# Attention of layer 1: a second output bank in the early steps, and a new order of values, low parts, swaps and ropes

## What is computed

```python
def sink_attend(q, k, v, sink, mask):
    s = jnp.einsum('...qkgd,...jkd->...kgqj', q, k).astype(jnp.float32) * (C_DH ** -0.5)
    if mask is not None:
        s = jnp.where(mask, s, -jnp.inf)
    sk = jnp.broadcast_to(sink.astype(jnp.float32)[:, :, None, None], s.shape[:-1] + (1,))
    p = jax.nn.softmax(jnp.concatenate([s, sk], axis=-1), axis=-1)[..., :-1]
    return jnp.einsum('...kgqj,...jkd->...qkgd', p.astype(v.dtype), v)

def odd_mixer(h, pos, k_cache, v_cache, w_in, b_in, w_out, sink):
    z = h @ w_in + b_in
    q, k, v = ...                      # 16 query heads, 2 key/value heads, 64 wide
    q, k = rope(q, pos), rope(k, pos)
    ...                                # each chunk of 64 queries sees 192 keys
    return o @ w_out, ...
```

## Time and profile before

| | us |
|---|---|
| median of 3 runs | 2476.39 (2475.01 to 2478.08) |
| profiled execution | 2472.65 |
| its span | 2470.9 |
| attention of layer 1, scores of batch 0 to the first product after the attention | 1411.9 to 1603.1 |
| PE busy over the span | 2385.7 |
| DVE, ACT, POOL busy over the span | 1408.4, 816.2, 216.2 |

### The profile page before, as it was taken

The page is one execution under the profiler, slowest core; times in us unless marked ns, Lnnn a source line. Parts: engine busy times, 40 slices in busy tenths (PEclk is TensorE's granted clock), DMA queues, the critical chain, the costliest instruction groups (busy, mean ns, idle before and its releaser), DMA issues.

```text
span 2470.9 us, 36737 instructions
## 1 busy us (share of the span) xinstructions
PE 2385.7 (97%) x15073; PEld 2296.2 (93%) x15073; DVE 1408.4 (57%) x2008; ACT 816.2 (33%) x1473; POOL 216.2 (9%) x147
## 2 busy tenths in 40 slices
PE   8998898999999999999999879999999999999998
PEld 7998677999999999999999857799999999999998
DVE  4445666665555655555574466666455555555557
ACT  5323566432222222222245465443222222222224
POOL 3435001000000000000040032200000000000003
PEclk9999999999999999999999989999999999999999
DMA  5112100211111111111002100021111111111101
GB/s 154 53 52 73 32 14 10 69 52 52 51 51 34 35 50 34 51 51 51 18 8 75 32 6 17 21 69 54 49 51 51 34 51 34 38 46 51 51 1 74
DMA packets 108291, 110.98 MB, mean 45 GB/s; under 512 B 3448, under 2 KB 98079, under 8 KB 108204
## 3 DMA queue, kind: packets, MB, share of 16 engines
q1 hardware_dynamic: 103268, 107.30, 13.7%
q10 hardware_dynamic: 4936, 2.47, 0.4%
HBM read 99.92 MB, written 9.42 MB: 44 GB/s over the span
## 4 chain that ended last, share of the span: by engine, by line
PE 89%; DVE 5%; ACT 3%; issue 1%; POOL 1%; DMA 0%; SPq 0%; ACTq 0%; POOLq 0%; DVEq 0%
PE PS L234 76%; PE PS L2395 2%; PE PS L1986 2%; PE PS L369 1%; PE PS L2377 1%; PE PS L2020 1%; PE PS L2332 1%; PE PS L2004 1%; PE PS L2227 1%; DVE nm L1414 1%; PE PS L2176 1%; DVE m L1697 1%; ACT E L1189 1%; ACT zs_e L828 1%; PE PS L1917 0%
## 5 line engine op out<-in xcount | busy, mean ns | idle before, releaser
L234 PE MATMUL PS<-xhi,uphi_f 128*128 128x364 f32 x2064 | 456.5, 330 | 0.9 <-issue 0.9
L234 PE MATMUL PS<-xhi,uplo_f 128*128 128x364 f32 x2064 | 455.1, 329 | 0.0
L234 PE MATMUL PS<-xlo,uphi_f 128*128 128x364 f32 x2064 | 455.1, 329 | 0.0
L234 PEld LDWEIGHTS PS<-xhi,uphi_f 128*128 128x128 f32 x2064 | 357.7, 188 | 2.4 <-issue 1.5
L234 PEld LDWEIGHTS PS<-xlo,uphi_f 128*128 128x128 f32 x2064 | 357.8, 188 | 0.0
L234 PEld LDWEIGHTS PS<-xhi,uplo_f 128*128 128x128 f32 x2064 | 357.8, 188 | 0.0
L1618 DVE TENSOR_TENSOR resid<-PS,resid 128x728 f32<-128x728 f32 x320 | 216.8, 720 | 181.6 <-PE PS L234 181.6
L234 PE MATMUL PS<-hhi_f,dhi_f 128*128 128x364 f32 (+1 forms) x1008 | 222.9, 330 | 2.2 <-DVE hlo_f L1289 2.2
L234 PE MATMUL PS<-hhi_f,dlo_f 128*128 128x364 f32 (+1 forms) x1008 | 222.9, 330 | 0.0
L234 PE MATMUL PS<-hlo_f,dhi_f 128*128 128x364 f32 (+1 forms) x1008 | 222.7, 329 | 0.0
L1028 ACT COPY edge<-ext_f 128x4 f32 (+1 forms) x86 | 17.1, 199 | 530.3 <-DVE ext_f L1544 530.3
(11 more groups left out here) (312 smaller groups left out, 3426.2 us busy)
## 6 DMA issues: line engine op xcount, KB each, us to landing
graw<-in_w_up SPq DMA_DIRECT2D x22, 1024.0 KB, 5.1
vraw<-in_w_up SPq DMA_DIRECT2D x22, 1024.0 KB, 5.1
draw<-in_w_down SPq DMA_DIRECT2D x22, 1024.0 KB, 5.0
wraw<-in_w_in_even SPq DMA_DIRECT2D x16, 512.0 KB, 4.1
wraw<-in_w_in_odd SPq DMA_DIRECT2D x10, 512.0 KB, 4.4
out_y_prompt<-yN SPq DMA_DIRECT2D x8, 512.0 KB, 2.7
xnat<-in_x_prompt SPq DMA_DIRECT2D x3, 1024.0 KB, 6.7
out_diff_k_prompt<-kNat ACTq DMA_DIRECT2D x4, 512.0 KB, 3.4
```

The costliest lines, as they stand in the source:

```text
L234: last = nc.tensor.matmul(PS[:, 3 * s + c, 0:width], w, x[:, a:a + width], start=(k == 0 and n == 0), stop=(k == nk - 1 and n == 2))
```

## The change

- **Output bank.** `out_bank(q)`: batches 1, 3, 5 and 7 write their output to bank 7, all others to bank 6. `out_free(q)` is the number of low parts that must have been taken before the values of batch q may start: for q = 2 to 8 those of batch q-2, from q = 9 on those of batch q-1 as before.
- **PE order.** In all steps the values of q-3 stand ahead of the transposes of q-2, and within the values the products with `PTr` ahead of those with `PTm`.
- **DVE order.** In steps 14 to 37 the low part of q-4 stands ahead of the maximum of q, and the addition of the first slice after the denominator. The exponentials now wait for `nm` alone, no longer for `snk`.
- **ACT order.** `fo_hi` and `op_first_hi` stand at the head of their step, ahead of the exponentials, not at its end. Their low parts on DVE stay at the end.
- **Last swap and rope.** The four swaps stand at the head of ACT's steps 1 to 4, one each; the three ropes at the end of DVE's steps 6, 7 and 8. Batch 9 waits for them as before.
- `FO_K`, `FO_GROUPS`, `FO_STEP` give the same 48 slices in the same steps and the same weight loads.

```diff
+        def out_bank(q):
+            return 7 if q % 2 and q < 2 * RT // FO_GROUPS else 6
+        def out_free(q):
+            before = [p for p in range(q) if out_bank(p) == out_bank(q)]
+            return before[-1] + 1 if before else 0
...
+        ROPE9 = {1: 0, 2: 1, 3: 2, 4: 3}
...
+            def last_swap(c):
+                if c == 0:
+                    reached(act, 1, "in_ev", 10)
+                    reached(act, 1, "in_rope", 8)
+                a = 32 * (c ^ 1)
+                last = identity(zs_o[32 * c:32 * c + 32, :], z_o[a:a + 32, :], bias=par[a:a + 32, 6, P_BIN + 7:P_BIN + 8])
+                if c == 3:
+                    last.then_inc(S("in_sw"), 1)
...
             for q in range(STEPS):
+                if q in ROPE9:
+                    last_swap(ROPE9[q])
+                if q in FO_READY:
+                    fo_hi(FO_READY[q])
+                if q in (NQ - 4, NQ - 2):
+                    op_first_hi(1, q // (NQ - 2))
                 if q < NQ:
                     odd_exps(q, (0, 1))
...
-                if q == 1:
-                    swap_bias(9)
...
             for q in range(STEPS):
-                if q - 1 in FO_AT:
-                    fo_add(FO_AT[q - 1][1])
+                slots = FO_AT.get(q, [[], []])
+                for j in FO_AT.get(q - 1, [[], []])[1]:
+                    fo_add(j)
+                if q >= 4 and q in FO_AT:
+                    odd_out_lo(q - 4)
                 if q < NQ:
                     odd_max(q)
-                if q >= 4:
+                if q >= 4 and q not in FO_AT:
                     odd_out_lo(q - 4)
-                if q in FO_AT:
-                    fo_add(FO_AT[q][0])
                 if 1 <= q <= NQ:
                     odd_den(q - 1)
+                for j in slots[0]:
+                    fo_add(j)
                 if 2 <= q < NQ + 2:
                     odd_probs_rest(q - 2)
-                if q == 1:
-                    query_rope(9)
+                if q - 4 in ROPE9 and q >= 6:
+                    last_rope(q - 6)
...
-                if q >= 1:
-                    pe.wait_ge(S("om_lo"), q)
+                if out_free(q):
+                    pe.wait_ge(S("om_lo"), out_free(q))
                 work = []
+                for c in query_chunks(t):
+                    work.append((c, PTr[:, v], (vS if c else v2N)[0:64, t, dims]))
...
                 if q < NQ:
                     odd_scores(q)
-                if q in FO_AT:
-                    fo_products(FO_AT[q][0])
-                if 2 <= q < NQ + 2:
-                    odd_probs(q - 2)
+                for j in slots[0]:
+                    fo_products(j)
                 if 3 <= q < NQ + 3:
                     odd_values(q - 3)
-                if q in FO_AT:
-                    fo_products(FO_AT[q][1])
+                if 2 <= q < NQ + 2:
+                    odd_probs(q - 2)
+                for j in slots[1]:
+                    fo_products(j)
```

More of the change, by code:

```diff
@@ L382, in window @@
             return [(slice(0, 64), 128, 192), (slice(64, 128), 64, 192)] if t == 0 else [(slice(0, ROWS[t]), 0, 192)]
-        FO = 6 * KT
+        FO_K = 2
         FO_START = 14
-        FO_AT = {q: [2 * (q - FO_START), 2 * (q - FO_START) + 1] for q in range(FO_START, FO_START + FO // 2)}
-        FO_UNITS = FO // 3
-        FO_READY = {10: 0, 11: 1}
-        FO_READY.update({FO_START + (3 * w - 4) // 2 + 1: w for w in range(2, FO_UNITS)})
+        FO_AT = {q: [[2 * (q - FO_START)], [2 * (q - FO_START) + 1]] for q in range(FO_START, FO_START + 24)}
+        FO_GROUPS = HK // FO_K
+        FO_UNITS = FO_GROUPS * KT
+        FO = 3 * FO_UNITS
+        FO_STEP = {j: q for q, slots in FO_AT.items() for js in slots for j in js}
+        FO_READY = {10: 0, 11: 1}
+        FO_READY.update({FO_STEP[3 * w - 4] + 1: w for w in range(2, FO_UNITS)})
+        ROPE9 = {1: 0, 2: 1, 3: 2, 4: 3}
[4 more added lines that the diff above has]
+            return before[-1] + 1 if before else 0
         OUTP = [dict(x=xn0, y=xn1, w=io["w_out_even"][0], gain=P_NF0, n=1, l=0, tag="op", ks=[0, 1, 2, 3], raw=wraw_h),
@@ L1197, in odd_sink @@
                 nq, v = ROWS[BATCHES[q][0]], q % 2
+                act.wait_ge(S("o_m"), 2 * q + 2)
                 nc.scalar.activation(es2[0:nq, v, :], snk2[0:nq, v, :], ACT.Exp).then_inc(S("o_es"), 1)
@@ L1775, in odd_out_lo @@
                 split_lo(xn1[1][:, 2 * b:2 * b + 2, rows_of(t)],
[L1776 removed]
+                         PS[:, out_bank(q), 0:256].rearrange("p (j q) -> p j q", j=2)[:, :, 0:ROWS[t]],
                          xn1[0][:, 2 * b:2 * b + 2, rows_of(t)]).then_inc(S("om_lo"), 1)
@@ L2371, in odd_values @@
                         work.append((c, PTm[0:64, v], v2N[0:64, 0, dims]))
-                for c in query_chunks(t):
-                    work.append((c, PTr[:, v], (vS if c else v2N)[0:64, t, dims]))
                 for n, (c, probs_t, vals) in enumerate(work):
                     for par_ in range(2):
-                        out = PS[64 * par_:64 * par_ + 64, 6, 0:256].rearrange("p (j q) -> p j q", j=2)[:, :, 64 * c:64 * c + 64]
+                        out = PS[64 * par_:64 * par_ + 64, out_bank(q), 0:256].rearrange("p (j q) -> p j q", j=2)[:, :, 64 * c:64 * c + 64]
                         last = nc.tensor.matmul(out, vals, probs_t[:, 2 * par_:2 * par_ + 2, 64 * c:64 * c + 64],
@@ L2387, in fo_products @@
                 if w % KT == 0 and c == 0:
-                    pe.wait_ge(S("om_lo"), RT * (w // KT + 1))
+                    pe.wait_ge(S("om_lo"), 2 * RT // FO_GROUPS * (w // KT + 1))
                 if j:
                     reached(pe, 1, "pq_ev", j)
-                for n in range(2):
-                    k = HK + 2 * (w // KT) + n
+                for n in range(FO_K):
+                    k = HK + FO_K * (w // KT) + n
                     x = [xn1[i][:, k, a:a + width] for i in range(2)]
@@ L2395, in fo_products @@
                         last = nc.tensor.matmul(PS[:, 7, 0:width], wt[:, w % 2, n, :], y,
-                                                start=(n == 0 and m == 0), stop=(n == 1 and m == 2))
+                                                start=(n == 0 and m == 0), stop=(n == FO_K - 1 and m == 2))
                 last.then_inc(S("pq_mm"), 1)
```

27 lines of the change are left out of this document (17 added, 10 removed).

## The result

The changed kernel takes 2472.56 us (median of 12 runs, 2468.99 to 2474.04), the one before, run beside it, 2477.53 us (12 runs): ratio 0.998, 95% interval 0.9971 to 0.9988. That is 5.0 us faster, 3 to 7 by the interval. The forecast was 9.5 us, and 2472.56 lies just outside its range (2472.5).

A forecast was written before the change was run, and what follows sets the result against it. Before step 14 PE waits, bound by the ring of values, scores, maximum and low part; then PE's own work counts. Gains of 8.7 before the slices and 0.8 in them, 9.5 us, took 2476.39 to 2466.9 us, range 2462.5 to 2472.5.

The forecast's parts named there:

- Steps 0 to 5: Start of layer 1's attention, swaps spread: ACT the bound at some 3.9 us a step, gain 9 to 10 us.
- Steps 6 to 8: Ropes spread: DVE the bound, three steps of 3.85 us, batch 9 at 1445.4 instead of 1454.1, gain 8.7 us.
- Steps 9 to 11: Batches 9 to 11, batch 9 being tile 0 with exponentials of 4.4 us: 11.0 us for three steps.
- Steps 12 and 13: Last steps before the slices: one bank again, transposes between values and next scores, 4.9 us each, 9.8 together.
- rival A: Clock stays low from PE's idle ahead of batch 9 until step 14: gain 3 us, 2473.4 us; chance 12%.
- Slices: Steps 14 to 37: earlier high parts gain, 1.2 us lost to changes of matmul shape, net gain 0.8 us.
- C: Slow start, PE at half clock until batch 6: 4 to 5 us less, gain 5, 2471.4 us; chance 7%.
- D: More gain: no clock lost ahead of batch 9, free shape changes, first slices never wait: 2463.1 us; chance 15%.
- B: The order costs more in the slices than all else gives: 3.7 us slower, 2480.1 us; chance 6%.
- batch 14 later than 1471: Sign that the forecast is wrong: scores of batch 14, forecast near 1466.3, start after 1471.

The follow-up runs named there:

- e1: The changed kernel with the three ropes moved ahead of the denominator in DVE's steps 6 to 8: 2470.0 us, ratio 0.9967 to the kernel before.
- e8: The changed kernel with 48 useless transposes on PE, ahead of batch 9's scores and behind the scores in steps 12 and 13: 2470.3 us, ratio 0.9969.
- e9: The changed kernel with two output banks until batch 10, and ropes and step 11's low part of the weights ahead of the denominator: 2463.3 us, ratio 0.9948.
- e4: The kernel before with the spread swaps and ropes alone, one output bank and the old orders: 2469.0 us, ratio 0.9959.

## Why the prediction was wrong

- **Direction and mechanism:** faster, for the swaps' and ropes' hole went. Right. The size was half: 5.0 instead of 9.5 us. (Before was measured again at 2477.5, 1.1 us above the median that the forecast started from. With it the forecast would be 2468.0 and its range 2463.6 to 2473.6, which holds the 2472.6; the gain is half of the forecast's all the same.)
- **Steps 0 to 5** (forecast: batch 5 about 18.1 us after batch 0): 18.7. Nearly right, but through PE at half clock between batches 3 and 4 (5.1 us) as much as through ACT. The forecast let ACT alone be the bound; that the number came out is partly luck.
- **Steps 6 to 8** (forecast: three DVE steps of 3.85 us, batch 9 at 33.5): 36.2. The step that failed: three DVE steps of 3.85 us each, a 2.55 us step without waits plus a rope of 1.3 us. I took the rope's time from a moment when POOL was idle and moved it to one when POOL is busy, and I left out DVE's own waits for the transposes. DVE took 13.3 us instead of 11.55, 1.7 more; meetings with POOL made about 1.6 of its 13.3. The other 1.0 us of the miss was there before the first of these steps: the scores of batch 6 were done at 22.8 us, not at 21.9. e1 gets it all back (33.2), about half of it by the place of the ropes.
- **Steps 9 to 11** (11.0 us): 11.0, batch 12 at 47.2.
- **Steps 12 and 13** (9.8 us): 12.7. The mechanism was forecast: one bank again, transposes in the ring. The term was mis-sized, as its parts were taken at full clock: 2.4 us for the half clock (e8). The other 0.5 has the size of the low part of the weights, which takes 0.7 us longer beside POOL in step 12; in e9 a shorter one gave 0.4. That an idle of 2.5 us costs clock stood in rival A, for batch 9 alone; in the changed kernel it happened in both steps of this ring, after idles of 2.6 and 1.9 us.
- **Slices** (127.2 us): 126.7; the cost of shapes was not there.
- **Rivals:** C had the gain that was measured, 5 us, but put the loss into a slow start, where only 0.6 us of it was. A had the cause of 2.4 us, but in other steps. Of D only the free changes of shape came, and B did not.
- **Sum:** 2.7 + 2.9 = 5.6 us more before the slices than forecast, 0.5 less in them. The forecast stretch was 181.6, measured 186.6. The result lies 2.1 us above the range that had 60%, 2464.5 to 2470.5; "batch 14 later than 1471" was named as what would show it wrong, and it is at 1411.9 + 59.9 = 1471.8.

Much of the gain was turned into new waits inside the same change: its early steps won 8.2 us by batch 5, and 5.1 of them were lost by batch 14.

## What to carry to other kernels

When an instruction moves, take its duration from its new neighbours, not its old ones: a VectorE instruction with two SBUF inputs beside a GpSimd one made one of them wait for the other here, and its place within a step decided whether they met. An experiment that moves an instruction changes both its neighbours and what stands ahead of it; read both from the timeline. Before work is put into a ring (values, transposes, scores here), ask whether the wait that hid it is really gone in every step; where it is not, it costs its full length, and at half clock nearly twice that (1.9 us instead of 1.0 for the transposes here). Switch from two buffers to one at the moment when the second is needed, not earlier.

## What the runs showed of the hardware

- POOL's scaling of 128x768 takes 1.47 us alone and, in the changed kernel and e4, 2.96 to 3.03 beside a rope that began 0.36 or 0.37 us after it; where the rope began 0.88 to 0.90 us after it, the rope took 1.71 to 1.73 us instead of 1.27 to 1.35. A 128x256 low part takes 0.41 us alone, 0.87 and 1.13 beside POOL.
- 48 useless transposes of the identity made the stretch 3.8 us shorter, with TensorE's granted clock at 1.00 over waits of about 2 us. 34 of them in a wait of 4.2 us gained nothing: the clock was 1.00 there and 0.55 in the five microseconds after 1425.
- TensorE's granted clock fell to 0.50 after idles of 2.5 and 2.6 us and again after one of 1.9 us; with idles of 0.9 us in each step of the kernel before it stayed at 1.00.
- A step with two more changes of matmul shape was 0.04 us shorter than the one with fewer.
